# Four residual norms of a two-layer hybrid step: the residual add on GpSimd instead of VectorE

## The chip, the cores and the metric

The kernel runs on one core of one Trainium2 chip. The metric is the device time of one execution in microseconds (us). Three runs of the kernel before took 2152.05, 2147.31 and 2153.11 us, the median is 2152.05.

## The reference

One step of a model of two layers over 512 prompt tokens and 8 single tokens (520 columns, called T), width 1024, all in float32. Layer 0 mixes with RWKV-7 and mLSTM heads side by side, layer 1 with retention. What surrounds the mixers is the same in both layers:

```python
def rmsnorm(x, g):
    xf = x.astype(jnp.float32)
    y = xf * lax.rsqrt(jnp.mean(xf * xf, axis=-1, keepdims=True) + RMS_EPS)
    return (y * g.astype(jnp.float32)).astype(x.dtype)
...
        h = h + rmsnorm(mix, g[1])
        f = jnp.square(jax.nn.relu(rmsnorm(h, g[2]) @ W['ffn_up'][li])) @ W['ffn_down'][li]
        h = h + rmsnorm(f, g[3])
        h = h + jax.nn.sigmoid(h @ W['ple_gate'][li]) * (p[li] @ W['ple_proj'][li])
```

The change is about the two lines `h = h + rmsnorm(...)` in each of the two layers: four norms in all.

## The kernel before

Activations lie transposed in SBUF: the width of 1024 is 8 tiles (KD) of 128 partitions, each with the 520 tokens as columns. `h` is one of two such buffers of 8 tiles (`h_a`, `h_b` in the profile, `hb[0]` and `hb[1]` in the code), `out` is the other one. Weights come from HBM in chunks of 128x1024 into `slot`; ScalarE rounds a chunk into `w_high` (L2120), VectorE takes the rest as `w_low` (L2124), and TensorE multiplies three pairs, high by high, low by high and high by low (L2136), six matmuls of 260 columns a k-step. The activations are split in high and low parts in the same way: `x_high` and `x_low` ahead of the FFN, `hidden_high` and `hidden_low` ahead of the gate GEMM. The order of the instructions on each engine is written out by hand; the engines wait for each other with counting semaphores.

One norm (n = 0 to 3) goes like this:

- While the GEMM ahead of it ends, ScalarE squares each output tile into `sqr` (L387, or L2218 in the FFN) and GpSimd sums the squares into `ss` (`pool_sum`, L394 and L397). TensorE turns the sum into a mean (`pe_postnorm`, L357), ScalarE takes the root (`act_rms`, L365), VectorE the reciprocal `rb` (`dve_rinv`, L369).
- `dve_residual` then does for each tile kt: a scale, `tmp = out * gain * rb` (L414), and an add, `h = h + tmp` (L417), which tells `s_h`. Both wait for their forerunner's semaphore. Two tiles later it makes the low part of the tile (the inner function `low`).
- In norms 0 and 2 (after the mixer, before the FFN; called FFN norms here) ScalarE's `act_prenorm` waits for `s_h` and makes `x_high` (L375) and the square (L376) of each tile; then `low` is L409 (`x_low`). TensorE sums the squares of all 8 tiles (`pe_prenorm`, L350) and goes on to the FFN's first GEMM.
- In norms 1 and 3 (after the FFN, before the gate; gate norms) ScalarE's `act_ple` waits for `s_h`, makes `hidden_high` (L2272), then copies a projection tile out of PSUM (L2275), and `low` is L405 (`hidden_low`). TensorE's `pe_proj` (L2264) makes 8 projection tiles into two buffers, so that tile mt waits for the copy of tile mt-2, and the gate GEMM follows it.

In the profile `tmp`, `sqr`, `ss` and `rt` are all parts of one tensor named `free`. GpSimd does little else: small copies of carried-over columns in the first GEMM (L1607, L1613), and products in the RWKV stage (L703, L705, L709).

Of the kernel before, what the change touches and what calls it, by code (L numbers as in the profile page):

```python
# [26 lines left out]
ALU = mybir.AluOpType  # L27
# [4 lines left out]
KD = D // P  # L32
# [173 lines left out]
def program(nc, stop=None, **dram):  # L206

    with ExitStack() as ctx:
# [3 lines left out]
        def sem(name):  # L212
            return ctx.enter_context(nc.semaphore(name))
# [27 lines left out]
        def tiles(t, n=KD, w=T):  # L241
            return t[:, 0:n * w].rearrange("p (k t) -> p k t", t=w)

        hb = [tiles(t) for t in hbuf]
# [6 lines left out]
        rb = rb_t[:, :]  # L251
# [4 lines left out]
        tmp = [tail.take(T), tail.take(T)]  # L256
# [7 lines left out]
        def V(name, i=0, n=1):  # L264
            a, _ = VEC[name]
            return vec[:, a + i:a + i + n]
# [21 lines left out]
        s_h = sem("h_ready")  # L288
        s_res = sem("residual_step")
# [100 lines left out]
        def pool_sum(pool, n):  # L390
            for mt in range(KD):
                pool.wait_ge(s_sq, 8 * n + mt + 1)
                if mt == 0:
                    nc.gpsimd.tensor_copy(ss, sqr[0]).then_inc(s_ss, 1)  # L394
                else:
                    pool.wait_ge(s_ss, 8 * n + mt)
                    nc.gpsimd.tensor_tensor(ss, ss, sqr[mt % 2], ALU.add).then_inc(s_ss, 1)  # L397

        def dve_residual(dve, n, out, h, gain, split=None):
            def low(kt):  # L400

                lyr, g = split
                if g is None:
                    dve.wait_ge(s_gh, 8 * lyr + kt + 1)
                    nc.vector.tensor_tensor(hl[:, kt, :], h[:, kt, :], hh[:, 8 + kt, :].bitcast(F32),  # L405
                                            ALU.subtract).then_inc(s_gl, 1)
                    return
                dve.wait_ge(s_xg, 8 * (2 * lyr + 1) + kt + 1)
                nc.vector.scalar_tensor_tensor(xl[:, kt, :], h[:, kt, :], V("norm_g", g * 8 + kt),  # L409
                                               xh[:, kt, :].bitcast(F32), ALU.mult, ALU.subtract).then_inc(s_xl, 1)  # L410
            for kt in range(KD):
                if split and kt >= 2:
                    low(kt - 2)
                nc.vector.scalar_tensor_tensor(tmp[0], out[:, kt, :], V("norm_g", gain * 8 + kt), rb,  # L414
                                               ALU.mult, ALU.mult).then_inc(s_res, 1)
                dve.wait_ge(s_res, 8 * n + kt + 1)
                nc.vector.tensor_tensor(h[:, kt, :], h[:, kt, :], tmp[0], ALU.add).then_inc(s_h, 1)  # L417
                dve.wait_ge(s_h, 8 * n + kt + 1)
            if split:
                low(KD - 2)  # L420
                low(KD - 1)


        ds = bass.ds
        half_b, xg_q = 4 * T, 4 * T
# [268 lines left out]
        def pool_rwkv(pool):  # L694
            def half(h):
                rd, ra, rl, b = rw[h]["dve"], rw[h]["act"], rw[h]["pool"], halves_of_heads[h]
                for g in range(NG):
                    def after(steps, name):
                        pool.wait_ge(*steps.at(name, g))
                    yield  # L700
                    yield
                    after(rd, "kp")
                    nc.gpsimd.tensor_tensor(b.rkb, uah(0, h, g), b.kp, ALU.mult).then_inc(*rl.step("rk"))  # L703
                    after(rl, "rk")
                    nc.gpsimd.tensor_tensor(b.rkb, b.rkb, bc(V("rk", 2 * h, 2), L), ALU.mult).then_inc(*rl.step("rkw"))  # L705
                    yield
                    yield
                    after(ra, "raw")
                    nc.gpsimd.tensor_tensor(b.nn, b.nn, mid(C("near"), 4), ALU.mult).then_inc(*rl.step("nn"))  # L709
                    for _ in range(12):  # L710
                        yield

            in_rounds(half)
# [352 lines left out]
        def pe_rwkv1(pe):  # L1066
# [41 lines left out]
            for j in range(4):  # L1108
                for b in range(NS):
# [24 lines left out]
            dve=["wia", "wca", "e0", "e1", "e2", "e3", "iwa", "mprev", "kh", "pt", "qi", "hd",  # L1134
                 "hr", "hb", "ho", "c0", "c1", "c2", "c3", "yc", "rinv", "yn", "out"],
# [466 lines left out]
        def pool_in0(pool):  # L1602
            with pool.Fori(0, 4) as i:
                for s in range(2):
                    t = 2 * i + s
                    pool.wait_ge(s_bank, t + 3)
                    nc.gpsimd.tensor_copy(cvo[:, ds(t, 1), :].squeeze(1),  # L1607
                                          ub[:, ds(t, 1), TP - 3:].squeeze(1)).then_inc(s_raw, 1)
            with pool.Fori(0, NA // 2) as i:
                for s in range(2):  # L1610
                    t = 2 * i + s
                    pool.wait_ge(s_bank, t + NB + 3)
                    nc.gpsimd.tensor_copy(sho[:, ds(t, 1), :].squeeze(1),  # L1613
                                          ua[:, ds(t, 1), TP:].squeeze(1)).then_inc(s_raw, 1)
# [46 lines left out]
        def pe_tiles(pe):  # L1661
# [87 lines left out]
            dve=["kt", "pt", "qd", "bn", "ag", "ri", "nm", "s"],  # L1749
# [540 lines left out]
        def dve_ple(dve, lyr, h, hn):  # L2290
            v = nc.vector
            _, t0, _, _, _ = GEMMS[f"gate{lyr}"]
            for mt in range(KD):
                e = sqr[mt % 2]
                if mt < KD - 2 or lyr == 0:
                    dve_low(dve, CHUNKS[f"gate{lyr}"], mt + 2)
                dve.wait_ge(s_bank, t0 + mt + 3)
                dve.wait_ge(s_pjc, 8 * lyr + mt + 1)
                v.tensor_tensor(e, e, hid[:, mt, :], ALU.mult).then_inc(s_pl, 1)
                dve.wait_ge(s_pl, 8 * lyr + mt + 1)  # L2300
                v.tensor_tensor(hn[:, mt, :], h[:, mt, :], e, ALU.add).then_inc(s_hn, 1)
# [26 lines left out]
        def _(sp):  # L2328
# [21 lines left out]
            def proj_weights(lyr):  # L2350
                _, t0, _, n, _ = GEMMS[f"up{lyr}b"]
                sp.wait_ge(s_tile, t0 + n)
                sp.dma_start(pjw[:, :], dram["pjw"][lyr]).then_inc(s_pj_w, 16)
# [157 lines left out]
        def _(dve):  # L2511
# [20 lines left out]
            dve_rinv(dve, 1)  # L2532
            dve.wait_ge(s_x2, 16)
            dve_residual(dve, 0, hb[1], hb[0], 1, (0, 2))
            dve_rinv(dve, 2)
            dve_ffn(dve, 0, hb[1])
            dve_rinv(dve, 3)
            dve_residual(dve, 1, hb[1], hb[0], 3, (0, None))
            dve_ple(dve, 0, hb[0], hb[1])
            dve.wait_ge(s_xg, 24)  # L2540
# [7 lines left out]
            for c in range(2):  # L2548
                dve_low(dve, FFN_CHUNKS[1], c)
            dve_rinv(dve, 5)  # L2550
            dve_residual(dve, 2, hb[0], hb[1], 5, (1, 6))
            dve_rinv(dve, 6)
            dve_ffn(dve, 1, hb[0])
# [4 lines left out]
        @block.gpsimd  # L2558
        def _(pool):
            pool_in0(pool)  # L2560
            pool_rwkv(pool)
            for n in range(4):
                pool_sum(pool, n)


INS = {"vec": (P, NVEC), "con": (P, NCON), "x": (P, KD * T), "w": (NSLAB, P, SLAB), "pjw": (2, P, KP * KD * P),
# [107 lines left out]
```

## Time and profile before

| | |
|---|---|
| median of three runs | 2152.05 us (2147.31 to 2153.11) |
| the profiled execution's own time | 2154.12 us |
| its span in the profile | 2152.3 us |
| TensorE busy, matmuls | 1975.4 us, 92% |
| VectorE busy | 998.9 us, 46%, 1493 instructions |
| ScalarE busy | 672.8 us, 31% |
| GpSimd busy | 72.3 us, 3%, 82 instructions |
| HBM read and written | 160.48 MB and 25.03 MB, 86 GB/s over the span |

PE is TensorE, DVE VectorE, ACT ScalarE and POOL GpSimd. The share of busy time is an average over stages with different limits; what a change in one stage is worth is read from the chain of waits in that stage, which leads from each instruction back to the one that released it. The span is the time between the first and the last instruction of the profiled execution; its own time is measured from outside and is 1.8 us more.

### The profile page before, as it was taken

What the parts mean: (1) busy time and instruction counts of PE and PEld (TensorE: products, weight loads), DVE (VectorE), ACT (ScalarE), POOL (GpSimd) and SP (SyncE); (2) the same over time, 40 slices, a digit from 0 to 9 for tenths busy, and PEclk for the clock granted to TensorE, in tenths of its full rate; (3) what the DMA queues carried; (4) which work ended last, traced back from release to release, by engine and by line L of the source; (5) the groups of instructions that cost most, each with busy time, mean ns of one, the idle gap of its engine ahead of it and who ended that gap; (6) DMA issues with size and microseconds to landing.
All of it is one profiled execution on the core that took longest, in us unless ns stands there. A gap on an engine that the chain in (4) does not pass through costs nothing.

```text
span 2152.3 us, 39908 instructions
## 1 busy us (share of the span) xinstructions
PE 1975.4 (92%) x16899; PEld 1805.8 (84%) x16899; DVE 998.9 (46%) x1493; ACT 672.8 (31%) x928; POOL 72.3 (3%) x82
## 2 busy tenths in 40 slices
PE   8988887888587999999899999999999799999989
PEld 7967775777265999999899976666999699999978
DVE  6546762555514442342266745555642643234244
ACT  4222214323113332332243123335432433233222
POOL 0000000111000000000100000000001000000000
PEclk9998985889678999999999999999999899999999
DMA  5202110000221222222313224444223122222221
GB/s 197 96 30 79 40 64 0 3 2 3 101 81 48 78 89 97 88 88 97 108 49 118 88 90 177 179 171 186 99 90 96 40 97 88 89 97 88 89 97 60
DMA packets 44750, 187.01 MB, mean 87 GB/s; under 512 B 5480, under 2 KB 5992, under 8 KB 39272
## 3 DMA queue, kind: packets, MB, share of 16 engines
q1 hardware_dynamic: 44648, 185.53, 25.1%
q8 instruction: 79, 1.29, 0.2%
q14 instruction: 23, 0.19, 0.0%
HBM read 160.48 MB, written 25.03 MB: 86 GB/s over the span
## 4 chain that ended last, share of the span: by engine, by line
PE 84%; DVE 10%; ACT 3%; issue 2%; POOL 0%; DMA 0%; DVEq 0%; POOLq 0%; SPq 0%; ACTq 0%
PE ps L2136 52%; PE ps L2019 7%; PE ps L332 3%; PE ps L727 2%; PE ps L1681 2%; PE ps L2084 1%; DVE h_a L1909 1%; PE ps L2094 1%; PE ps L2078 1%; DVE free L414 1%; PE ps L1705 1%; PE ps L350 1%; PE ps L1667 1%; PE ps L2074 1%; DVE rb L369 1%
## 5 line engine op out<-in xcount | busy, mean ns | idle before, releaser
L2124 DVE TENSOR_TENSOR w_low<-slot,w_high 128x1024 fp32r<-128x1024 f32 x240 | 293.5, 1224 | 495.0 <-ACT w_high L2120 494.9
L2120 ACT ACTIVATE w_high<-slot 128x1024 fp32r<-128x1024 f32 x240 | 254.0, 1059 | 797.6 <-PE ps L2136 709.5
L2136 PE MATMUL ps<-x_high,w_high 128*128 128x260 f32 x1600 | 323.3, 283 | 1.1 <-issue 1.1
L2136 PE MATMUL ps<-x_high,w_low 128*128 128x260 f32 x1600 | 322.9, 283 | 0.0
L2136 PE MATMUL ps<-x_low,w_high 128*128 128x260 f32 x1600 | 322.4, 283 | 0.0
L2136 PE MATMUL ps<-hidden_high,w_low 128*128 128x260 f32 x1536 | 309.5, 283 | 0.0
L2136 PE MATMUL ps<-hidden_high,w_high 128*128 128x260 f32 x1536 | 309.4, 283 | 0.0
L2136 PE MATMUL ps<-hidden_low,w_high 128*128 128x260 f32 x1536 | 309.0, 283 | 0.0
L2136 PEld LDWEIGHTS ps<-x_high,w_high 128*128 128x128 f32 x1600 | 247.7, 189 | 1.8 <-issue 1.5
L2136 PEld LDWEIGHTS ps<-x_high,w_low 128*128 128x128 f32 x1600 | 247.2, 189 | 0.0
L2136 PEld LDWEIGHTS ps<-x_low,w_high 128*128 128x128 f32 x1600 | 246.6, 189 | 0.0
L2136 PEld LDWEIGHTS ps<-hidden_high,w_high 128*128 128x128 f32 x1536 | 236.9, 188 | 0.1
L2136 PEld LDWEIGHTS ps<-hidden_high,w_low 128*128 128x128 f32 x1536 | 236.8, 188 | 0.0
L2136 PEld LDWEIGHTS ps<-hidden_low,w_high 128*128 128x128 f32 x1536 | 236.2, 188 | 0.0
L2233 DVE SCALAR_TENSOR_TENSOR free<-ps,rb 128x520 f32<-128x520 f32 x64 | 44.8, 700 | 172.4 <-PE ps L2136 172.4
L2019 PE MATMUL ps<-x_high,w_high 128*128 128x260 f32 x448 | 109.8, 327 | 0.0
L2019 PEld LDWEIGHTS ps<-x_high,w_high 128*128 128x128 f32 x448 | 72.4, 193 | 33.1 <-issue 31.6
L2019 PE MATMUL ps<-x_low,w_high 128*128 128x260 f32 x448 | 91.7, 287 | 0.0
L2019 PE MATMUL ps<-x_high,w_low 128*128 128x260 f32 x448 | 91.7, 287 | 0.0
L2019 PEld LDWEIGHTS ps<-x_high,w_low 128*128 128x128 f32 x448 | 70.8, 193 | 0.0
L2019 PEld LDWEIGHTS ps<-x_low,w_high 128*128 128x128 f32 x448 | 70.7, 193 | 0.0
L350 PE MATMUL ps<-big,con 128*128 128x260 f32 x128 | 41.4, 479 | 31.5 <-ACT big L376 31.4
(555 smaller groups left out, 2634.4 us busy)
## 6 DMA issues: line engine op xcount, KB each, us to landing
slot<-in_w SPq DMA_DIRECT2D x240, 512.0 KB, 3.8
h_a<-in_rst SPq DMA_DIRECT2D x16, 1024.0 KB, 4.9
out_rst_o<-h_a SPq DMA_DIRECT2D x16, 1024.0 KB, 3.9
slot<-in_w SPq DMA_DIRECT2D x2, 2048.0 KB, 8.4
h_a<-in_x SPq DMA_DIRECT2D x4, 520.0 KB, 5.2
h_a<-in_x SPq DMA_DIRECT2D x1, 2080.0 KB, 7.6
out_y<-h_a SPq DMA_DIRECT2D x8, 260.0 KB
con<-in_con SPq DMA_DIRECT2D x1, 2062.0 KB, 16.0
```

The costliest lines, as they stand in the source:

```text
L332: mm = pe.matmul(ps[:, 2 * par + hf, 0:HALF], slot[s][:, at:at + P], rhs(kt, hf), start=(kt == 0), stop=(kt == nk - 1))
L350: mm = pe.matmul(ps[:, 4 + hf, 0:HALF], C("mean_d"), hid[:, 24 + kt, hf * HALF:(hf + 1) * HALF], start=(kt == 0), stop=(kt == KD - 1))
L369: nc.vector.reciprocal(rb, rt).then_inc(s_rb, 1)
L414: nc.vector.scalar_tensor_tensor(tmp[0], out[:, kt, :], V("norm_g", gain * 8 + kt), rb, ALU.mult, ALU.mult).then_inc(s_res, 1)
L727: mm = pe.matmul(ps[sub_rows[c], b_, off + k.start:off + k.stop], lhs(par, j)[sub_rows[c]], rhs(par, j)[sub_rows[c]], start=start, stop=stop)
L1667: mm = pe.matmul(ps[0:36, 6 + hf, 0:HALF], V("wif", 36 * kt, 36), x[:, kt, hf * HALF:(hf + 1) * HALF].bitcast(F32), start=(kt == 0 and x i ...
L1681: mm = pe.matmul(ps[:, hf, 0:HALF], w[m % 2][:, at], y(kt, hf), start=(kt == 0 and n == 0), stop=(kt == KD - 1 and n == 2))
L2019: mm = pe.matmul(ps[:, 2 * par + hf, 0:HALF], w[m % 2][:, at], y(kt, hf), start=(kt == 0 and w is wh and lo == 0), stop=(kt == 7 and w is wl))
L2120: nc.scalar.activation(wh[c % 2], raw[c % 4], ACT.Copy).then_inc(s_wh, 1)
L2124: nc.vector.tensor_tensor(wl[c % 2], raw[c % 4], wh[c % 2].bitcast(F32), ALU.subtract).then_inc(s_wl, 1)
L2136: mm = pe.matmul(ps[:, 2 * par + hf, 0:HALF], w[c % 2][:, at], y(kt, hf), start=(start and kt == 0 and w is wh and y is x), stop=(stop and ...
L2233: v.scalar_tensor_tensor(two(tmp[m % 2]), bank(m % 2), 0.0, two(rb), ALU.max, ALU.mult).then_inc(s_bank, 1)
```

## The change

The add of each tile moves from VectorE to GpSimd, in a new function `pool_residual` that GpSimd runs after each `pool_sum`. VectorE writes the scaled output to two buffers in turn (`tmp[0]`, `tmp[1]`), and from the third tile on it waits, before it writes one, until the add of two tiles earlier is done. It no longer waits for its own scale and add.

```diff
@@ -411,15 +411,19 @@
             for kt in range(KD):
                 if split and kt >= 2:
                     low(kt - 2)
-                nc.vector.scalar_tensor_tensor(tmp[0], out[:, kt, :], V("norm_g", gain * 8 + kt), rb,
+                if kt >= 2:
+                    dve.wait_ge(s_h, 8 * n + kt - 1)
+                nc.vector.scalar_tensor_tensor(tmp[kt % 2], out[:, kt, :], V("norm_g", gain * 8 + kt), rb,
                                                ALU.mult, ALU.mult).then_inc(s_res, 1)
-                dve.wait_ge(s_res, 8 * n + kt + 1)
-                nc.vector.tensor_tensor(h[:, kt, :], h[:, kt, :], tmp[0], ALU.add).then_inc(s_h, 1)
-                dve.wait_ge(s_h, 8 * n + kt + 1)
             if split:
                 low(KD - 2)
                 low(KD - 1)
 
+
+        def pool_residual(pool, n, h):
+            for kt in range(KD):
+                pool.wait_ge(s_res, 8 * n + kt + 1)
+                nc.gpsimd.tensor_tensor(h[:, kt, :], h[:, kt, :], tmp[kt % 2], ALU.add).then_inc(s_h, 1)
 
         ds = bass.ds
         half_b, xg_q = 4 * T, 4 * T
@@ -2561,6 +2565,7 @@
             pool_rwkv(pool)
             for n in range(4):
                 pool_sum(pool, n)
+                pool_residual(pool, n, hb[n // 2])
```

VectorE's instructions in the first norm, before (L369 is the reciprocal, L414 a scale, L417 an add, L409 an `x_low`):

```order
L369 RECIPROCAL rb<-free 128x520
L414 SCALAR_TENSOR_TENSOR free<-h_b,vec,rb 128x520
L417 TENSOR_TENSOR h_a<-h_a,free 128x520
L414 SCALAR_TENSOR_TENSOR free<-h_b,vec,rb 128x520
L417 TENSOR_TENSOR h_a<-h_a,free 128x520
L409 SCALAR_TENSOR_TENSOR x_low<-h_a,vec,x_high 128x520
L414 SCALAR_TENSOR_TENSOR free<-h_b,vec,rb 128x520
```

The same place with the change (L416 is the scale now):

```order
L369 RECIPROCAL rb<-free 128x520
L416 SCALAR_TENSOR_TENSOR free<-h_b,vec,rb 128x520 x2
L409 SCALAR_TENSOR_TENSOR x_low<-h_a,vec,x_high 128x520
L416 SCALAR_TENSOR_TENSOR free<-h_b,vec,rb 128x520
L409 SCALAR_TENSOR_TENSOR x_low<-h_a,vec,x_high 128x520
```

Two scales stand in a row at the start, and then scales and low parts take turns; the adds have left VectorE. On GpSimd, with the change, behind the last RWKV product (L713, which was L709), through the second norm:

```order
L713 TENSOR_TENSOR free<-free,con 128x512
L394 COPY free<-free 128x520
L397 TENSOR_TENSOR free<-free 128x520 x7
L426 TENSOR_TENSOR h_a<-h_a,free 128x520 x8
L394 COPY free<-free 128x520
L397 TENSOR_TENSOR free<-free 128x520 x7
L426 TENSOR_TENSOR h_a<-h_a,free 128x520 x8
```

L426 is the new add: eight of them behind the sums of each norm, and ahead of the sums of the next.

## Rows read from the trace of the kernel before

**Rows 1.** The page: busy time of the engines; and the chain that ended last, by engine.

```profile
PE 1975.4 (92%) x16899; PEld 1805.8 (84%) x16899; DVE 998.9 (46%) x1493; ACT 672.8 (31%) x928; POOL 72.3 (3%) x82
...
PE 84%; DVE 10%; ACT 3%; issue 2%; POOL 0%; DMA 0%; DVEq 0%; POOLq 0%; SPq 0%; ACTq 0%
```

**Rows 2.** Chain of waits, first norm: start us, us, what ran in it.

```profile
678.35 0.77 DVE free L414
...
690.98 0.68 DVE free L414
...
691.68 0.71 DVE h_a L417
...
693.88 0.71 DVE h_a L417
...
694.62 0.02 ACT x_high L375
...
695.93 2.10 PE ps L350 x4
```

**Rows 3.** Chain of waits, second norm.

```profile
1079.88 0.77 DVE free L414
...
1088.62 0.71 DVE h_a L417
...
1090.76 0.71 DVE h_a L417
...
1091.49 0.64 ACT hidden_high L2272
...
1092.67 2.02 PE ps L2264 x8
```

**Rows 4.** Timeline: start of the gate GEMM and the last two low parts.

```profile
1094.34 0.59 PE L2136 MATMUL ps<-hidden_high,w_high 128*128 128x260 f32 x2
...
1095.78 1.38 DVE L405 TENSOR_TENSOR hidden_low<-h_a,hidden_high 128x520 fp32r<-128x520 f32 x2
```

**Rows 5.** Groups of VectorE in the first norm: x_low (xcount, busy us, mean ns).

```profile
L409 DVE SCALAR_TENSOR_TENSOR x_low<-h_a,vec,x_high 128x520 fp32r<-128x520 f32 x8 | 6.1, 760 | 0.8 <-ACT big L376 0.5
```

**Rows 6.** Line L414 (scales): ns min/median/max, first and last start.

```profile
L414 DVE SCALAR_TENSOR_TENSOR free<-h_b,vec,rb x16: 752/755/760, 678.4 to 1094.3; 128x520 f32<-128x520 f32 x16
L414 DVE SCALAR_TENSOR_TENSOR free<-h_a,vec,rb x16: 752/754/760, 1687.7 to 2101.2; 128x520 f32<-128x520 f32 x16
```

**Rows 7.** Line L397 (GpSimd's sums): ns min/median/max.

```profile
L397 POOL TENSOR_TENSOR free<-free x28: 1277/1309/1861, 629.0 to 2079.3; 128x520 f32<-128x520 f32 x28
```

**Rows 8.** Timeline, a tile of out1: VectorE and GpSimd at once.

```profile
1657.29 0.58 ACT L387 ACTIVATE free<-ps 128x520 f32<-128x520 f32 x1
...
1657.41 1.23 DVE L2124 TENSOR_TENSOR w_low<-slot,w_high 128x1024 fp32r<-128x1024 f32 x1 [4.52 <-ACT w_high L2120]
...
1657.95 1.86 POOL L397 TENSOR_TENSOR free<-free 128x520 f32<-128x520 f32 x1 [9.65 <-ACT free L387]
```

**Rows 9.** Timeline of the RWKV stage, and line L553's ns min/median/max.

```profile
365.51 0.80 POOL L703 TENSOR_TENSOR h_a<-big,h_b 128x256 f32<-128x256 f32 x1 [51.10 <-DVE h_b L549]
365.68 0.91 DVE L553 SCALAR_TENSOR_TENSOR h_a<-h_b,h_a 128x256 f32<-128x256 f32 x1
...
L553 DVE SCALAR_TENSOR_TENSOR h_a<-h_b,h_a x4: 415/416/906, 365.7 to 497.5; 128x256 f32<-128x256 f32 x4
```

**Rows 10.** Stretches behind norms 0 to 2; from the timeline, statistics matmuls in norm 2.

```profile
core 0: us, PE busy (x) PEld busy (x) DVE busy (x) ACT busy (x) POOL busy (x), PEclk, DMA share, GB/s
698.00:701.00 3.00, 3.00 (x16) 3.00 (x15) 2.30 (x1) 0.60 (x1) 0.00 (x0) 0.50 0.00 0
1094.30:1101.00 6.70, 6.70 (x56) 6.66 (x55) 2.78 (x5) 2.13 (x4) 0.00 (x0) 1.00 0.01 2
1706.00:1710.00 4.00, 4.00 (x34) 3.97 (x33) 2.96 (x1) 0.60 (x1) 0.00 (x0) 1.00 0.00 0
...
1698.63 1.14 PE L350 MATMUL ps<-big,con 128*128 128x260 f32 x4 [1.06 <-ACT big L376]
```

## The prediction

> **What bounds the kernel now.** I read the page first. TensorE is busy 92% of the span and carries 84% of the chain that ended last; VectorE is busy 46% and has 10% of that chain; GpSimd is busy 3% [rows 1]. So the kernel is a stream of matmuls, and VectorE counts only where TensorE has nothing to do. The next view is the chain of waits around the first norm. There VectorE leads without a break: the reciprocal, then scale (L414), add (L417), x_low (L409), scale, add and so on, until ScalarE's copy and square of the last tile let the last statistics matmuls and then the FFN start [rows 2]. The chain of the second norm looks the same up to ScalarE's copy L2275, which releases the last projection tile, and the gate GEMM follows it [rows 3, 4]. A norm holds 8 scales of 755 ns, 8 adds of 0.70 us and 8 low parts, in an FFN norm of 760 ns, in a gate norm of 0.69 (two in 1.38) [rows 2, 4, 5, 6]. Norms 2 and 3 repeat this at the second layer: the 16 scales there have the same median, 754 against 755 ns [rows 6]. So the four norms are four places where VectorE and what feeds it set the time, and a moved instruction counts in full there.
>
> Before, the first norm takes from the start of scale 0 at 678.35 to the end of add 7 at 693.88 + 0.71 = 694.59, that is 16.2 us; its steady step is one tile per 2.20 us (add 6 at 691.68, add 7 at 693.88) [rows 2]. In the second norm, what decides is add 5: from 1079.88 to 1090.76 + 0.71 = 1091.47, 11.6 us, with a step of 2.14 us (from add 4 at 1088.62) [rows 3]. Behind add 5 stand the copies L2272 and L2275 on ScalarE, then the last projection tile and the gate at 1094.3 [rows 3, 4]. Tiles 6 and 7 have slack there: their low parts end at 1095.78 + 1.38 = 1097.2, while the gate's first tile, at six matmuls a k-step and 6.70 us for 56 matmuls, asks for k-step 7 only at 1094.3 + 7 x 0.72 = 1099.3 [rows 4, 10].
>
> **The change, part by part.**
>
> 1. Removed from VectorE: 8 adds of 0.70 us per norm, 32 in all, with two semaphore gaps of 0.03 us around each. All lie on the path. Alone that would be worth 8 x 0.73 = 5.8 us a norm.
>
> 2. Added to GpSimd: 8 two-input adds of the same 128x520 shape per norm. GpSimd already does such an add at L397: 1277 ns at least, 1309 in the median, 1861 at most [rows 7]. The semaphore from another engine costs it 0.08 us (1657.29 + 0.58 to 1657.95) [rows 8]. GpSimd is idle otherwise: the sums of a norm (L397) stand before its statistics matmuls and so before its reciprocal, so nothing queues behind. These adds are on the path in VectorE's place, since ScalarE's copies and squares wait for each.
>
> 3. What the two engines do to each other. In out1, the GpSimd sum is issued while VectorE runs L2124, which reads two SBUF tensors. The sum then takes 1.86 us and ends 1.17 us behind VectorE's instruction (1657.95 + 1.86 against 1657.41 + 1.23) [rows 8]; six of out1's seven adds are like this. So it stood still until VectorE was through. The other direction is seen in the RWKV stage: L553, a scalar_tensor_tensor of the very kind of scale and x_low, takes 415 ns by itself, and 906 ns (printed 0.91) where GpSimd's L703 is running; it ends 0.28 us after L703 (365.68 + 0.91 = 366.59 against 365.51 + 0.80 = 366.31) [rows 9]. L555 does the same behind L705. So a waiting instruction seems to have its start-up done and to pay only its columns: for 520 columns 0.28 x 520/256 = 0.57 us, my estimate. All three instructions left in a norm, scale, low and add, read two SBUF tensors, hence I take it that the add runs beside neither of the other two. The change then takes 0.70 us from VectorE and puts 1.28 us in its place on what is still one queue.
>
> 4. FFN norms (0 and 2). From the first scale: scale 0 ends at 0.76, scale 1 right behind it at 1.43 (0.68 when back to back [rows 2]). Add 0 stands until 1.43 and ends 1.17 later, at 2.6; add 1 at 3.8. From here a step is: low held by the add, ending 0.57 behind it; scale 0.68; semaphore 0.08; add 1.28; together 2.6 us, against 2.20 before. Add 7 ends at 3.8 + 6 x 2.6 = 19.4, against 16.2: **+3.2 us each**.
>
> 5. Gate norms (1 and 3). The start is the same, 3.8 for add 1. The low part needs only ScalarE's one copy of 0.64 us (L2272) before it rather than two, so the pieces fit closer together: the step lies between the three held lengths with no gap, 0.57 + 0.57 + 1.17 = 2.3 us, and the 2.6 above. I take 2.4. Add 5 ends at 3.8 + 4 x 2.4 = 13.4, against 11.6: **+1.8 us each**. The slack of 2.1 us of tiles 6 and 7 mostly remains, because the gate moves too.
>
> 6. The second buffer and the waits on h: before scale kt, VectorE waits for add kt-2. That one is already over when the low part of tile kt-2 is, as that reads it; it costs nothing. Dropped waits: counted in 1. No DMA is issued or moved by the change.
>
> The sum is 2 x 3.2 + 2 x 1.8 = **+10.0 us**. Against the profiled execution's own 2154.12 us that is 2164.1; the median of the runs is 2152.05, 2.1 us below it, and the same sum gives **2162.0**. The lower bound is a step of 2.3 in all norms (perfect handover): 17.6 - 16.2 = +1.4 and 13.0 - 11.6 = +1.4, in total +5.6; the upper end is in the third rival.
>
> By the Trainium skill, "SBUF — State Buffer", section "Who interferes with whom", a VectorE instruction with two SBUF inputs contends with a GpSimd instruction that reads SBUF, and the second to issue "fully blocks" until the first is done. The trace agrees that one waits for the other (0.906 against 0.415 us), though it shows that a held instruction loses less than its whole length.
>
> **The rivals.**
>
> *No conflict for these instructions* (not slower). If a scale and an add could run together, add 0 ends at 0.83 + 1.28 = 2.1, add 1 at 3.4. In an FFN norm two tiles then take 1.30 (ScalarE and its semaphore, 694.62 to 695.93 [rows 2]) + 0.76 + 0.68 + 0.08 + 1.28 = 4.1 us; add 7 ends at 15.7, -0.5 us. In a gate norm two tiles take 0.67 + 0.70 + 0.68 + 0.08 + 1.28 = 3.4, add 5 ends at 10.2, -1.4 us. In total -3.8 us, 2148.3: still inside 0.3%. For it: GpSimd's add was never seen against an instruction of 520 columns with these tiles. Against it: the two places where they meet [rows 8, 9]: each time one of the two gets longer. It decides from an FFN step of 2.2 us down. Chance 0.13.
>
> *The clock falls at more places.* After norm 0 TensorE is granted 0.50 (1.2 GHz) from 698 to 701 us, and after norms 1 and 2 (norm 3 is as norm 1) it is granted 1.00 (2.4 GHz) [rows 10]. The last group of four statistics matmuls in norm 0 took 2.10 us [rows 2], one in norm 2 1.14 behind a gap of 1.06 [rows 10]. With longer gaps the three others may fall too. A fall costs 0.96 us in that group and half of the 3.0 us behind it, some 2.5 us: at two more places +5.0, in all +15.0 us and 2167.0. For it: the gaps grow. Against it: norm 2 has the same steps of VectorE as norm 0, hence the same gaps, and did not fall. Chance 0.15.
>
> *A held instruction starts over.* If it paid its full 0.76 us or so behind the add, steps are 2.8 and 2.6: add 7 at 20.6 and add 5 at 14.2, +4.4 and +2.6, in total +14.0 us, 2166.0. L553 speaks against it (0.28, not 0.42). Chance 0.07. The skill's words in the section named above, that the loser waits for the whole instruction, would read this way if taken literally; the trace disagrees with that reading.
>
> *The forecast*, steps of 2.4 to 2.6: chance 0.60. The remaining 0.05 is for a gain that I do not see.
>
> **How the numbers follow.** A measurement of this kernel can tell 0.3%, or 6.5 us, from no change. The forecast is +10.0 us with a spread of about 3 from its steps and 2 from the runs (2147.31 to 2153.11), so some 0.13 of its 0.60 falls under 6.5. Slower: 0.47 + 0.15 + 0.07 = 0.69. Same: 0.13 + 0.13 = 0.26. Faster: 0.05. The range holds 2151.5 to 2169: below, the perfect handover (+5.6, or 2157.7) with the runs' own spread and some of the no-conflict case; above, the two dearer rivals with 3 us. That leaves out most of the no-conflict case and of the gains.
>
> **What would show it.** In the changed profile the adds on GpSimd at the norms should take 1.28 us where VectorE is still and 1.7 or more for add 0; x_low or scale should show durations of 1.1 to 1.8 us where an add is running, against 0.76. From the first scale to the end of add 7 should be 19.4 us in norms 0 and 2, and to the end of add 5 13.4 us in norms 1 and 3. Adds and scales that overlap at undisturbed lengths would refute step 3, and with it the sign. TensorE's granted clock behind norms 1 to 3 should stay at 1.00; a fall there is the second rival. A time under 2155.6 means that the steps were shorter than 2.3 us or that the path ran elsewhere.

## The result, and the profile after

| | before | with the change |
|---|---|---|
| median | 2152.05 us (2147.31 to 2153.11, 5 runs) | 2167.01 us (2159.82 to 2172.62, 5 runs) |
| ratio | | 1.0063, 95% interval 1.0039 to 1.0086 |
| the profiled execution's own time | 2154.12 us | 2159.82 us |
| its span | 2152.3 us | 2158.0 us |

The change makes the kernel slower by 0.4% to 0.9%. Six more runs of it, in the experiments, gave a median of 2167.92 us and a ratio of 1.0079 (1.0052 to 1.0106).

The page of the changed kernel, the lines that answer to [rows 1]:

```profile
PE 1976.1 (92%) x16899; PEld 1805.4 (84%) x16899; DVE 999.9 (46%) x1461; ACT 673.0 (31%) x928; POOL 118.4 (5%) x114
...
PE 85%; DVE 9%; ACT 3%; issue 2%; POOL 1%; DMA 0%; DVEq 0%; SPq 0%; ACTq 0%
```

VectorE's busy time has not fallen, although 32 instructions left it (998.9 before, 999.9 now): what it no longer spends on adds it spends held, that is, an instruction has been issued and counts as busy while it waits for GpSimd's. GpSimd's grew by 46 us.

The timeline of the first norm of the changed kernel (start us, us, engine, line), its start and one step; it answers to [rows 2]:

```profile
670.86 1.43 DVE L416 SCALAR_TENSOR_TENSOR free<-h_b,vec,rb 128x520 f32<-128x520 f32 x2
671.69 2.97 POOL L426 TENSOR_TENSOR h_a<-h_a,free 128x520 f32<-128x520 f32 x2 [6.73 <-DVE free L416]
...
681.22 1.29 POOL L426 TENSOR_TENSOR h_a<-h_a,free 128x520 f32<-128x520 f32 x1 [1.31 <-DVE free L416]
681.24 1.83 DVE L409 SCALAR_TENSOR_TENSOR x_low<-h_a,vec,x_high 128x520 fp32r<-128x520 f32 x1
...
682.99 0.75 DVE L416 SCALAR_TENSOR_TENSOR free<-h_b,vec,rb 128x520 f32<-128x520 f32 x1
...
683.82 1.28 POOL L426 TENSOR_TENSOR h_a<-h_a,free 128x520 f32<-128x520 f32 x1 [1.31 <-DVE free L416]
683.83 1.82 DVE L409 SCALAR_TENSOR_TENSOR x_low<-h_a,vec,x_high 128x520 fp32r<-128x520 f32 x1
```

The add of tile 4 (L426, GpSimd) runs from 681.22 to 682.51. The low part L409 is issued 0.02 us after it and ends at 683.07, 1.82 us long instead of 0.76, and 0.56 behind the add. The scale behind it ends at 683.74, and 0.08 later the next add starts: one tile in 2.60 us. This is the pattern from add 4 on; adds 2 and 3 end 3.32 and 1.93 us after the add ahead of them, 2.6 in the mean. The line summaries show which instructions are ever held in norms 0 and 1: most of the low parts of the FFN norm, and of a gate norm some scales, low parts and adds (the highest values), not all:

```profile
L409 DVE SCALAR_TENSOR_TENSOR x_low<-h_a,vec,x_high x8: 751/1487/1828, 674.7 to 691.6; 128x520 fp32r<-128x520 f32 x8
```

```profile
L416 DVE SCALAR_TENSOR_TENSOR free<-h_b,vec,rb x16: 747/753/1784, 670.9 to 1091.1; 128x520 f32<-128x520 f32 x16
```

```profile
L405 DVE TENSOR_TENSOR hidden_low<-h_a,hidden_high x8: 685/899/1798, 1079.0 to 1094.9; 128x520 fp32r<-128x520 f32 x8
```

```profile
L426 POOL TENSOR_TENSOR h_a<-h_a,free x16: 1277/1289/1732, 671.7 to 1092.9; 128x520 f32<-128x520 f32 x16
```

(Minimum, median and maximum in ns.) The gate norm's timeline shows who goes first when both want in:

```profile
1080.64 0.69 DVE L405 TENSOR_TENSOR hidden_low<-h_a,hidden_high 128x520 fp32r<-128x520 f32 x1
1080.80 1.68 POOL L426 TENSOR_TENSOR h_a<-h_a,free 128x520 f32<-128x520 f32 x1 [1.31 <-DVE free L416]
1081.25 1.78 DVE L416 SCALAR_TENSOR_TENSOR free<-h_b,vec,rb 128x520 f32<-128x520 f32 x1
...
1083.11 1.28 POOL L426 TENSOR_TENSOR h_a<-h_a,free 128x520 f32<-128x520 f32 x1 [0.63 <-DVE free L416]
1083.18 1.77 DVE L405 TENSOR_TENSOR hidden_low<-h_a,hidden_high 128x520 fp32r<-128x520 f32 x1
```

The low part is there first (1080.64 to 1081.33), so the add issued at 1080.80 takes 1.68 us; the scale issued at 1081.25 comes behind the add, not ahead of it, and ends at 1083.03, 0.55 after it. In these rows they are served in the order in which they arrive. Strict taking of turns would give the same here; these rows don't tell the two apart.

To follow all four norms in all kernels I measure each from the start of its first scale to the start of the first matmul of the next GEMM. Before: 19.11, 14.46, 18.36 and 14.46 us, together 66.4. With the change: 22.29, 16.50, 22.29 and 16.51, together 77.6. That is +11.2 us. TensorE's granted clock behind the norms, as in [rows 10]:

```profile
core 0: us, PE busy (x) PEld busy (x) DVE busy (x) ACT busy (x) POOL busy (x), PEclk, DMA share, GB/s
693.20:697.00 3.80, 3.80 (x19) 3.70 (x18) 2.61 (x1) 0.60 (x1) 0.00 (x0) 0.51 0.00 0
1092.00:1098.00 6.00, 6.00 (x50) 5.94 (x49) 3.34 (x3) 2.26 (x4) 1.60 (x2) 1.00 0.01 3
1708.80:1712.50 3.70, 3.70 (x24) 3.60 (x23) 2.42 (x1) 0.60 (x1) 0.00 (x0) 0.74 0.00 0
2107.00:2113.00 6.00, 6.00 (x51) 5.97 (x50) 3.16 (x3) 2.27 (x4) 1.42 (x2) 1.00 0.00 1
```

Behind norm 2 it is at 0.74 in the mean of the stretch now, where it was at 1.00: there the FFN (with all that follows) takes 381.65 us up to the next norm's first scale instead of 380.82, and the last statistics matmuls 2.10 us instead of 1.14. In the norm itself that is 0.75 us (22.29 - 18.36 = 3.93, against 3.18 in norm 0), and is in the 11.2 already, so the norms and what follows them make +12.0 us.

### The profile page after: what moved, and what is told of

Same layout as the page of the kernel before. It is cut to its first block, busy times and chain, and to the rows that moved or that the text cites. A ratio compares the mean times of both kernels' runs of the same rounds, so it can differ in the third digit from the quotient of the medians.

```text
span 2158.0 us, 39880 instructions
## 1 busy us (share of the span) xinstructions
PE 1976.1 (92%) x16899; PEld 1805.4 (84%) x16899; DVE 999.9 (46%) x1461; ACT 673.0 (31%) x928; POOL 118.4 (5%) x114
## 4 chain that ended last, share of the span: by engine, by line
PE 85%; DVE 9%; ACT 3%; issue 2%; POOL 1%; DMA 0%; DVEq 0%; SPq 0%; ACTq 0%
PE ps L2140 52%; PE ps L2023 7%; PE ps L1685 3%; PE ps L332 3%; PE ps L731 2%; PE ps L2088 1%; DVE h_a L1913 1%; PE ps L2098 1%; PE ps L350 1%; PE ps L2082 1%; PE ps L1709 1%; PE ps L1671 1%; PE ps L2078 1%; DVE rb L369 1%; PE ps L2035 1%
## 5 line engine op out<-in xcount | busy, mean ns | idle before, releaser
L2140 PEld LDWEIGHTS ps<-x_low,w_high 128*128 128x128 f32 x1600 | 246.9, 189 | 0.0
L350 PE MATMUL ps<-big,con 128*128 128x260 f32 x128 | 46.6, 526 | 34.6 <-ACT big L376 34.6
L350 PEld LDWEIGHTS ps<-big,con 128*128 128x128 f32 x128 | 31.4, 259 | 48.4 <-ACT big L376 34.6
```

What stands on the lines that cost most here:

```text
L350: mm = pe.matmul(ps[:, 4 + hf, 0:HALF], C("mean_d"), hid[:, 24 + kt, hf * HALF:(hf + 1) * HALF], start=(kt == 0), stop=(kt == KD - 1))
L2140: mm = pe.matmul(ps[:, 2 * par + hf, 0:HALF], w[c % 2][:, at], y(kt, hf), start=(start and kt == 0 and w is wh and y is x), stop=(stop and ...
```

## The experiments

Each has 6 to 12 runs, beside 12 to 35 of the kernel before. The table has the lengths of the four norms in each profile, their sum against the 66.4 of before, and what was measured. "Elsewhere" is the rest of the span; before it is 2085.9, and in the first profile of the change 2080.4.

| kernel | norm 0, 1, 2, 3 (us) | sum against before | median (us) | ratio to before (95%) | elsewhere |
|---|---|---|---|---|---|
| ffn_norms | 22.29, 14.45, 22.29, 14.46 | +7.1 | 2162.61 | 1.0047 (1.0028 to 1.0067) | 2083.3 |
| gate_norms | 18.35, 16.50, 19.09, 16.51 | +4.1 | 2161.34 | 1.0041 (1.0026 to 1.0055) | 2091.0 |
| beside_add | 25.47, 14.47, 25.45, 14.46 | +13.5 | 2171.64 | 1.0092 (1.0073 to 1.0111) | 2094.5 |
| beside_memset | 19.09, 14.46, 18.36, 14.46 | 0.0 | 2154.50 | 1.0012 (0.9998 to 1.0026) | 2082.6 |
| low_last_vector | 14.35, 13.14, 14.34, 13.14 | -11.4 | 2143.16 | 0.9942 (0.9921 to 0.9963) | 2083.6 |
| low_last_gpsimd | 17.26, 14.44, 17.24, 14.43 | -3.0 | 2150.12 | 0.9989 (0.9967 to 1.001) | 2088.5 |
| scale_first | 20.70, 15.94, 20.91, 15.94 | +7.1 | 2161.05 | 1.0025 (1.0003 to 1.0047) | 2085.9 |
| one_buffer | 22.69, 17.76, 22.70, 17.75 | +14.5 | 2167.87 | 1.0065 (1.0042 to 1.0088) | 2085.0 |
| psum_scale | 13.46, 14.44, 13.45, 14.45 | -10.6 | 2145.82 | 0.9966 (0.9942 to 0.9989) | 2089.3 |
| change_again | 22.29, 16.50, 22.29, 16.51 | +11.2 | 2167.92 | 1.0079 (1.0052 to 1.0106) | 2083.9 |
| each_best | 13.45, 13.14, 13.45, 13.14 | -13.2 | 2139.98 | 0.9928 (0.99 to 0.9956) | 2087.9 |
| low_last_vector_2 | 14.34, 13.14, 14.34, 13.14 | -11.4 | 2142.44 | 0.9942 (0.9921 to 0.9963) | 2085.7 |

The norms' lengths come back to 0.02 us for one order of instructions, but for the clock: an FFN norm of before takes 18.36 us when its last statistics matmuls run at full clock and 19.1 when they run at half. What is elsewhere, above all in the mixers ahead of the first norm, differs by up to 14 us (2080.4 to 2094.5) between profiled executions of these kernels, all of which have the same code there. So a mechanism is judged by the lengths, and the medians say what comes of it.

### Half of the change

```diff
+            if n % 2 == 0:
...
+            else:
...
             for n in range(4):
                 pool_sum(pool, n)
-                pool_residual(pool, n, hb[n // 2])
+                if n % 2 == 0:
+                    pool_residual(pool, n, hb[n // 2])
```

This is ffn_norms against the changed kernel; the first branch has the change's loop, the other the loop of before. In gate_norms the condition is `n % 2 == 1`.

> The adds on GpSimd in norms 0 and 2 only; norms 1 and 3 as before. Theory 1 (GpSimd's add and VectorE's two-SBUF-input instructions take turns, and each norm pays for itself): from the first scale to the first matmul of the next GEMM 22.3 us in norms 0 and 2 and 14.5 in norms 1 and 3, against 19.1, 14.5, 18.4, 14.5 before; +7.1 us from these, 8 to 9 with a fall of TensorE's clock behind norm 2. Theory 2 (most of the 15 us between the medians comes from the clock granted in the mixers, ahead of the first norm): the median lies anywhere between +0 and +15 whatever is moved, and the stretch ahead of the first norm differs by as much as the total.

> The adds on GpSimd in norms 1 and 3 only. Theory 1: 16.5 us from the first scale to the gate's first matmul in norms 1 and 3 and the lengths of before in norms 0 and 2; +4.1 us in all. Theory 2: as for the other half, no relation to the number of adds moved; the two halves do not add up to the whole.

Each norm has the length that it has in the whole change or before, whatever the other norms do: 7.1 + 4.1 = 11.2. Only the half clock has moved: in gate_norms, whose norms 0 and 2 have the code of before, it is norm 2 that ends with it (19.09) and norm 0 that does not (18.35). So which of two such norms it is does not depend on the change alone. The theory that the time lies in the mixers' clock has no support in the lengths. The median of ffn_norms is 10.6 us up (6.0 to 14.4 by its interval), and 7.1 lies in that. But the median of gate_norms is 5.6 to 11.8 us up, more than its norms' 4.1; its profile has 5 us more elsewhere, in the stretches ahead of norm 0 and of norm 2, which hold no changed instruction. I leave open where they come from.

### Something on GpSimd beside the old order

Both keep the adds on VectorE and give GpSimd one instruction per tile in norms 0 and 2, whose result nobody reads.

```diff
+        def pool_beside(pool, n):
+            for kt in range(KD):
+                pool.wait_ge(s_res, 8 * n + kt + 1)
+                if kt:
+                    pool.wait_ge(s_beside, 4 * n + kt)
+                nc.gpsimd.tensor_tensor(tmp[1], sqr[0], sqr[1], ALU.add).then_inc(s_beside, 1)
```

In beside_memset the last line is `nc.gpsimd.memset(tmp[1], 0.0)`. In both, VectorE waits for the eighth of them behind its last low part.

> The kernel before, with its adds on VectorE, and in norms 0 and 2 a GpSimd add of the same shape beside each tile, whose result nobody reads. Theory 1 (taking turns): each GpSimd add holds VectorE for some 1.0 to 1.17 us, so the step of an FFN norm goes from 2.20 to about 3.2 us, x_low or the scales show 1.7 us and more, +7 us per norm, +14 in all. Rival (the loss of the change is only that GpSimd's add is slow itself and on the path): VectorE's durations stay at 0.70 to 0.76 us, step 2.20, +0 us.

> As beside_add, but the GpSimd instruction beside each tile is a memset of the same 128x520 tile, which reads nothing. Theory 1a (what the two share is the reading of SBUF): VectorE keeps its durations, step 2.20, 0 us. Theory 1b (any GpSimd instruction on SBUF holds VectorE): some 0.4 us more per tile, +3 us per norm, +6 in all.

The low part in norm 0 of beside_add, with a tile's add on VectorE (L418), the idle add on GpSimd (L431) and the low part (L410); then one tile's add and GpSimd's memset in beside_memset, and the summaries of its low parts and memsets:

```profile
688.42 0.70 DVE L418 TENSOR_TENSOR h_a<-h_a,free 128x520 f32<-128x520 f32 x1
688.47 1.80 POOL L431 TENSOR_TENSOR free<-free 128x520 f32<-128x520 f32 x1 [1.31 <-DVE free L415]
...
689.16 1.67 DVE L410 SCALAR_TENSOR_TENSOR x_low<-h_a,vec,x_high 128x520 fp32r<-128x520 f32 x1
...
L410 DVE SCALAR_TENSOR_TENSOR x_low<-h_a,vec,x_high x8: 748/1669/1671, 686.0 to 706.3; 128x520 fp32r<-128x520 f32 x8
```

```profile
687.05 0.70 DVE L418 TENSOR_TENSOR h_a<-h_a,free 128x520 f32<-128x520 f32 x1
687.07 0.53 POOL L431 MEMSET free<- 128x520 f32 x1 [1.67 <-DVE free L415]
```

```profile
L410 DVE SCALAR_TENSOR_TENSOR x_low<-h_a,vec,x_high x8: 759/760/760, 681.2 to 695.7; 128x520 fp32r<-128x520 f32 x8
```

```profile
L431 POOL MEMSET free<- x16: 532/532/539, 678.9 to 1699.9; 128x520 f32 x16
```

A GpSimd add whose result nobody uses (the eighth ends at 705.81, ahead of the start of the last low part at 706.30, behind which VectorE waits for it) makes the low part 0.9 us longer and the step 3.11 us instead of 2.20, +6.4 and +7.1 us a norm (the idle adds start at 685.36 and 688.47). Its median is 20 us up, some 5 more than the norms (13.5) and the half clock behind both of them (1.3) account for; here too a part stays open. So the loss of the change is not only that its add is slow and on the path; the add also holds what runs beside it. A memset, which reads nothing, runs in the middle of VectorE's add (687.07 to 687.60 against 687.05 to 687.75), and neither gets longer; the norms are as before, and the median is within the noise of before. It is over before the low part starts, so it was tried beside the adds alone. What only writes does not take part, then; that it is the reading which is shared is the plain explanation, and psum_scale below tests it from VectorE's side.

### Other orders with the adds on GpSimd

scale_first puts the scale ahead of the low part:

```diff
             for kt in range(KD):
-                if split and kt >= 2:
-                    low(kt - 2)
                 if kt >= 2:
                     dve.wait_ge(s_h, 8 * n + kt - 1)
                 nc.vector.scalar_tensor_tensor(tmp[kt % 2], out[:, kt, :], V("norm_g", gain * 8 + kt), rb,
                                                ALU.mult, ALU.mult).then_inc(s_res, 1)
+                if split and kt >= 2:
+                    low(kt - 2)
```

> The change with the scale of tile k ahead of the low part of tile k-2 on VectorE. Then the next add's operand no longer stands behind a held low part: step 0.57 + 0.6 + 1.17 = 2.35 us instead of 2.6 (FFN norms), 2.35 instead of 2.45 (gate norms). FFN norms 20.7 us, gate norms 16.1; 4 us faster than the change, 7 slower than before. Rival (the order of the two makes no difference, since all three take turns in any order): 22.3 and 16.5 as with the change.

The lengths are 20.7 and 15.9: the order matters much as worked out, 1.4 to 1.6 us in an FFN norm and 0.6 in a gate norm against the change. Its sum is +7.1 us against before, and the median +8.5, with an interval from +0.6 to +10.

one_buffer uses `tmp[0]` alone, and a scale waits for the add just before it (`if kt >= 1: dve.wait_ge(s_h, 8 * n + kt)`).

> The change with one buffer: each scale waits for the add before it. Theory 1: in an FFN norm the scale of tile k+1 stands behind add k anyway (a step is low 0.57, scale 0.68, 0.08, add 1.28), so only the start gets longer, 22.7 instead of 22.3; in a gate norm the step goes from 2.45 to 2.6, 17.2 instead of 16.5. +2 us against the change. Rival (the two buffers let scale and add overlap, and carry the change): a step longer by 0.7 us in all norms, +20 us.

The FFN norms took 22.7 as expected, the gate norms 17.8 instead of 17.2. The second buffer, one of the two things that the change does, is worth 0.4 us in an FFN norm and 1.3 in a gate norm, not 0.7 us a tile: scale and add hardly overlap in any case. By the medians the two kernels can't be told apart (one_buffer is 15.3 us up, the change 15 and 16).

### Low parts last

```diff
             for kt in range(KD):
-                if split and kt >= 2:
-                    low(kt - 2)
...
-            if split:
-                low(KD - 2)
-                low(KD - 1)
+            for kt in range(KD):
+                low(kt)
```

> The kernel before, adds on VectorE, but the 8 low parts of a norm stand behind all its scales and adds. Theory 1 says that what counts in a norm is the order on the shared queue, and that the low parts are needed late: step 1.53 us (scale and add), add 7 ends at 12.2 us from the first scale, statistics end near 14.7, the low part of tile k at 12.3 + 0.68 x (k + 1), always ahead of the GEMM's k-step (0.72 us each). FFN norms 15 us instead of 18.4 to 19.1, gate norms 13 instead of 14.5, -10 to -11 us in all. Rival (the low parts become the bound: the GEMM waits at each k-step, or the reciprocal behind them comes too late): the norms get shorter, but the GEMM behind them loses the same, 0 to -4 us.

> The change (adds on GpSimd) with the 8 low parts behind all scales. Scales and adds still take turns: a step of 0.57 to 0.68 + 1.17 = 1.75 to 1.9 us, add 7 at 15.2, FFN norms 17.7 to 18.5 us, gate norms 14.4: about the times of before, -2 to +1 us, and 10 us slower than the same order with the adds on VectorE. Rival (no conflict between scale and add): a step of 1.28, and the same time as low_last_vector within 2 us.

The chain of waits at the end of the first norm of low_last_vector, and the eight low parts and the FFN's first matmuls in its timeline:

```profile
689.01 0.71 DVE h_a L415
...
690.38 0.63 ACT big L376
...
691.06 1.14 PE ps L350 x4
692.20 7.80 PE ps L2133 x65
```

```profile
689.75 5.46 DVE L409 SCALAR_TENSOR_TENSOR x_low<-h_a,vec,x_high 128x520 fp32r<-128x520 f32 x8
...
691.85 0.59 PE L2133 MATMUL ps<-x_high,w_high 128*128 128x260 f32 x2
```

With the adds on VectorE the step is 1.53 us, the last add ends at 689.72, 12.2 us from the first scale, and the FFN starts at 691.85 while the low parts run until 695.21. The GEMM behind it is not longer for that (380.81 us up to the next norm). In the gate norms the projection is the bound now: its matmuls lead the chain for 10.79 us without a break, and the norm takes 13.14 us. With the adds on GpSimd the same order has 17.25 (17.7 to 18.5 were expected) and 14.4: scale and add take turns, 3.6 us for two tiles. That is 8.4 us more than with the adds on VectorE by the lengths, and 7.0 by the medians:

```profile
685.29 2.44 DVE L414 SCALAR_TENSOR_TENSOR free<-h_b,vec,rb 128x520 f32<-128x520 f32 x2 [1.17 <-POOL h_a L423]
...
687.14 2.97 POOL L423 TENSOR_TENSOR h_a<-h_a,free 128x520 f32<-128x520 f32 x2 [0.64 <-DVE free L414]
```

(One line holds two scales or two adds there.) Before, and in the change, the low parts stood between the adds although nobody needed them yet. Putting them last was worth more than any place of the adds: -11.4 us in the norms, and medians 9.4 and, in the repeat, 11.7 us down.

### Letting both engines read

psum_scale is low_last_gpsimd, with the reciprocal of norms 0 and 2 in PSUM:

```diff
-            nc.vector.reciprocal(rb, rt).then_inc(s_rb, 1)
+            if r in (1, 5):
+                nc.vector.reciprocal(ps[:, 6:8, 0:HALF], two(rt)).then_inc(s_rb, 1)
+            else:
+                nc.vector.reciprocal(rb, rt).then_inc(s_rb, 1)
...
+                r_b = ps[:, 6:8, 0:HALF] if n % 2 == 0 else two(rb)
+                nc.vector.scalar_tensor_tensor(two(tmp[kt % 2]), two(out[:, kt, :]), V("norm_g", gain * 8 + kt), r_b,
                                                ALU.mult, ALU.mult).then_inc(s_res, 1)
```

> low_last_gpsimd with one difference: in norms 0 and 2 the reciprocal is written to two free PSUM banks and the scale reads it from there, so that the scale has one SBUF tensor input and one from PSUM. Theory 1, narrowed (only a VectorE instruction with two SBUF tensor inputs takes turns with a GpSimd add): in norms 0 and 2 add and scale overlap at their undisturbed lengths, 1.28 and 0.7 to 0.76 us, the adds stand back to back, ScalarE's 1.35 us per tile is the next bound, and these norms take 14.3 to 15.5 us instead of 17.25; norms 1 and 3 stay at 14.4. Rival (any VectorE instruction that reads SBUF takes turns with GpSimd): scales of 1.7 us and adds in turn as in low_last_gpsimd, 17.2.

The scales of psum_scale, with `ps` (FFN norms) and with `rb` in SBUF (gate norms), and the eight adds of the first norm in its timeline:

```profile
L418 DVE SCALAR_TENSOR_TENSOR free<-h_b,vec,ps x8: 751/756/757, 683.3 to 691.7; 128x520 f32<-128x520 f32 x8
L418 DVE SCALAR_TENSOR_TENSOR free<-h_b,vec,rb x8: 746/755/1769, 1077.6 to 1089.1; 128x520 f32<-128x520 f32 x8
```

```profile
684.11 10.48 POOL L427 TENSOR_TENSOR h_a<-h_a,free 128x520 f32<-128x520 f32 x8 [6.74 <-DVE free L418]
685.43 0.73 ACT L378 ACTIVATE x_high<-h_a,vec 128x520 fp32r<-128x520 f32 x1 [6.21 <-POOL h_a L427]
685.43 0.75 DVE L418 SCALAR_TENSOR_TENSOR free<-h_b,vec,ps 128x520 f32<-128x520 f32 x1 [0.73 <-POOL h_a L427]
...
686.67 0.73 ACT L378 ACTIVATE x_high<-h_a,vec 128x520 fp32r<-128x520 f32 x1
686.67 0.76 DVE L418 SCALAR_TENSOR_TENSOR free<-h_b,vec,ps 128x520 f32<-128x520 f32 x1 [0.49 <-POOL h_a L427]
```

With one of its two tensors in PSUM no scale is longer than 757 ns, while with both in SBUF they reach 1769. Eight adds take 10.48 us: they start 1.24 to 1.25 us apart, seven of them 1.28 to 1.31 long, and only the last is held, for 1.76, by a low part. The FFN norm takes 13.46 us against 17.26 in low_last_gpsimd and 14.35 in low_last_vector. It is 0.8 to 2.0 us shorter than I expected, because ScalarE, like the adds that it waits for, keeps a step of 1.25 us (685.43 to 686.67), not 1.35. The scales of norms 1 and 3 have the same form with `rb` in SBUF, and they are held, so it is the place of the operand that counts. GpSimd's adds pay after all in an FFN norm, by 0.9 us against low_last_vector, once VectorE reads no second tensor from SBUF beside them. The Trainium skill states this in "SBUF — State Buffer", section "Who interferes with whom": an instruction of VectorE with at most one SBUF input, outside the two-port performance modes, does not contend with GpSimd. The trace agrees (757 ns at most against 1769).

### The best of both, and two repeats

each_best takes the FFN norms of psum_scale and the gate norms of low_last_vector (in a gate norm TensorE's projection holds the banks that the reciprocal would need).

> Low parts last in all norms; in norms 0 and 2 the adds on GpSimd with the reciprocal in PSUM (as in psum_scale), in norms 1 and 3 the adds on VectorE (as in low_last_vector). Theory 1 (each norm pays for itself): lengths 13.46, 13.14, 13.46, 13.14, together 53.2 us against 66.4 before and 55.0 in low_last_vector; -13 us against before, -2 against low_last_vector. Rival (what is gained in the norm is lost behind it, since the reciprocal of the next statistics comes later behind the low parts): the GEMM behind norms 0 and 2 gets longer than the 380.8 us it takes at full clock, and the gain is that of low_last_vector or less.

> low_last_vector again, on the same chip as each_best. Lengths 14.35, 13.14, 14.34, 13.14 again, -11 us against before from the norms; the median 8 to 12 us under that of before. Rival (the first result was a lucky grant of the clock in the mixers): -5 us or less.

> The changed kernel again, with five more rounds beside the kernel before. Theory 1: the four norms account for 11.2 us and TensorE's half clock behind norms 0 and 2 for up to 2 more, so with more runs the difference settles at 11 to 13 us, and the norms have the lengths 22.3, 16.5, 22.3, 16.5 again. Rival (the change also costs something outside the norms): 15 us or more, with a stretch outside that is longer every time.

each_best has the lengths 13.45 and 13.14 and the lowest median, 2139.98 us, a ratio of 0.9928 (0.99 to 0.9956). The GEMM behind norm 0 takes 380.83 us: nothing is lost behind the norm. By the lengths it is 1.8 us ahead of low_last_vector_2 on the same chip, by the medians 2.5, but the intervals of the two overlap, so only the lengths show it. low_last_vector came back with the same ratio. change_again has the norms of the change to the hundredth, 381.80 us behind norm 2, and elsewhere it is no longer than before in all (2083.9). Its median is still 16 us up, where 11 to 13 were expected, though its interval reaches down to 11.2; the rival expectation, a stretch outside that is longer every time, does not show in its profile either. See below.

## Why the prediction was right

Forecast were 2162.0 us and slower; measured are 2167.01 and slower, inside the range.

- **Steps 1 and 2**, the adds on GpSimd at 1.28 us and on the path: right (1277 ns at least, 1288 or 1289 in the median).
- **Step 3**, taking turns, and a held instruction paying only its columns: right. A low part ends 0.56 us behind the add (forecast 0.57), add 0 takes 1.73 (671.69 to 673.42), forecast 1.77. beside_add and psum_scale show it by an added and a removed conflict. The rival *no conflict* is out by the first; the rival *starts over* by 0.56 against 0.76.
- **Step 4**, a step of 2.6 us: 2.60 (681.22 to 683.82), add 7 at 690.28, 19.42 us from the first scale, forecast 19.4. The step as described starts with add 4; adds 2 and 3 came 3.32 and 1.93 us after their forerunners, which the forecast did not have, and that they make up two steps of 2.6 together is luck.
- **Step 5**, 2.4 us, was a choice between 2.3 and 2.6, and its size is right: two tiles take 4.91 us (1083.11 against 1088.02 for the add of the same turn), 2.45 each; add 5 ends at 13.62, forecast 13.4. The picture behind the 2.3, every instruction held and no gap, is not what happens: of two tiles one scale, one low part and one add are held (1.78, 1.77 and 1.68 us), and the other three run at 0.75, 0.69 and 1.28. The gate norms cost 2.04 us rather than 1.8.
- **Step 6**, the second buffer free of cost: right, and it is worth 0.4 to 1.3 us a norm.
- **The rival of the clock** came true at one of the three places: norm 2 now ends at half clock, which costs 0.75 us in it and 0.83 behind it. I had it as a rival at 0.15 with two places, and 2.5 us for each; behind the gate norms the clock stayed full. That its 2167.0 is the measured median is chance: it brought 1.6 us, not 5. My argument against it, that norm 2 did not fall before, read one group of matmuls only. Norm 2 of before has two slowed groups (1.83 and 1.88 us) and is back at full clock for its last:

```profile
1700.83 1.83 PE L350 MATMUL ps<-big,con 128*128 128x260 f32 x4 [1.06 <-ACT big L376]
1703.03 1.88 PE L350 MATMUL ps<-big,con 128*128 128x260 f32 x4 [0.37 <-ACT big L376]
1705.23 1.14 PE L350 MATMUL ps<-big,con 128*128 128x260 f32 x4 [0.32 <-ACT big L376]
```

  With the change the last two groups of norm 2 are these; the three groups ahead of them took 2.02, 2.10 and 2.00 us:

```profile
1704.72 1.14 PE L350 MATMUL ps<-big,con 128*128 128x260 f32 x4 [0.59 <-ACT big L376]
...
1707.30 2.10 PE L350 MATMUL ps<-big,con 128*128 128x260 f32 x4 [1.44 <-ACT big L376]
```

- **The sum** was +10.0; norms and clock account for +12.0 in the profiles, 0.5 of the difference from the gate norms and 1.6 from the clock. The medians say +15 and +16, with intervals of +8.4 to +18.5 and +11.2 to +22.8. The 12.0 lies in both. Whether the rest is chance or something outside the norms stays open: neither of the two profiles of the change is longer elsewhere (2080.4 and 2083.9 against 2085.9), but a profile is one execution, and these two are the shortest of theirs (2159.82 and 2163.30 us). The mean granted clock of the runs gives a hint. Among the 93 runs of the kernel before beside the experiments, the time falls by some 1.7 us for each 0.001 of it, my estimate by a straight line through them (the three fastest, 2143 to 2144 us, have 0.947 to 0.949, the three slowest, all 2165, have 0.936). The median of the 11 runs of the change is 0.938 against 0.942 there. A part of this comes from the norms themselves, where the clock is lower while TensorE waits (0.58 in the first norm of the change against 0.68 before), so it does not show what the rest is.

## What to carry to other kernels

Moving an instruction to an idle engine gains only if that engine can run beside the one it relieves: look in the trace for a place where the two meet, and read the durations there before counting the busy share. Here two tensor inputs in SBUF on both sides made one queue of the two engines, and one operand in PSUM split it again. Before moving work elsewhere, ask which of the instructions between two links of the chain is needed now: putting the eight low parts behind the adds, on the same engine, brought what the move did not.

## What the runs showed of the hardware

- Where VectorE's and GpSimd's instructions both read two SBUF tensors, in the norms of these kernels, they run one after the other in order of arrival (or in strict turns, which the rows don't tell from it). A held one ends 0.55 to 0.57 us (VectorE, 0.76 alone) or 1.14 to 1.17 us (GpSimd, 1.28 alone) behind the other at 520 columns, as if its start-up were done by then. A GpSimd memset of the same tile (532 ns) beside VectorE's adds does not take part.
- One row of before fits neither order of arrival nor strict turns. In the mixers a small GpSimd copy stands 3.19 us while three of VectorE's long two-input instructions pass it back to back:

```profile
292.88 1.20 DVE L1323 TENSOR_TENSOR big<-free,con 8x1024 f32<-8x1024 f32 x1
...
293.23 3.19 POOL L1613 COPY h_a<-big  x1 [11.72 <-DVE big L1581]
...
294.01 1.21 DVE L1325 TENSOR_TENSOR h_b<-h_b,h_a 128x1024 f32<-128x1024 f32 x1
...
295.15 1.21 DVE L2124 TENSOR_TENSOR w_low<-slot,w_high 128x1024 fp32r<-128x1024 f32 x1
...
296.29 1.20 DVE L1329 TENSOR_TENSOR h_b<-h_b,ps 128x1024 f32<-128x1024 f32 x1
```

  The copy ends at 296.42, just behind the third of them (296.36), while the fourth, which reads `ps` in PSUM, runs. A copy beside such instructions was not tried by itself, so this stays open.
- A group of four statistics matmuls takes 1.14 us at full clock and 2.10 at half. The last group was at half clock in both FFN norms of the change (in both its profiles) and of ffn_norms, one_buffer and beside_add; in one of the two in before, beside_memset and gate_norms; in none where the low parts stand last. The length of a gap alone does not decide it: in gate_norms the gaps ahead of the last four groups are 1.05 or 1.06 us in both FFN norms, and the last group takes 1.14 us in norm 0 and 2.10 in norm 2:

```profile
698.32 1.14 PE L350 MATMUL ps<-big,con 128*128 128x260 f32 x4 [1.05 <-ACT big L376]
...
1710.81 2.10 PE L350 MATMUL ps<-big,con 128*128 128x260 f32 x4 [1.06 <-ACT big L376]
```

  Where the last group kept the full clock, what follows the norm is shorter too: 380.8 us up to norm 1 in low_last_vector, against 382.4 before. A shorter norm so brings a little more than its own length.
